# First two projection streams on x times the norm weight, with the token's factor applied when the sums are evacuated

## The reference, cut to what matters

```python
def rms_norm(x, g):
    xf = x.astype(jnp.float32)
    y = xf * lax.rsqrt(jnp.mean(xf * xf, axis=-1, keepdims=True) + EPS)
    return (y * g.astype(jnp.float32)).astype(x.dtype)
...
        h = rms_norm(x, norm_g[l])
        proj = h @ w_in[l]
        q, kv, g_logits, z_a, uv, z_b, merge_logits = jnp.split(proj, SPLIT_IDX, axis=-1)
```

## Time and profile before

| | |
|---|---|
| median of three runs | 2229.52 us |
| the profiled execution's own time | 2230.15 us |
| its span | 2228.4 us |
| TensorE busy | 2199.2 us (99%) |
| VectorE busy | 1545.2 us (69%) |
| ScalarE busy | 1080.6 us (48%) |
| GpSimd busy | 417.1 us (19%) |
| mean DMA rate | 173 GB/s |

### The profile page before, as it was taken

One profiled execution on the slowest core, in us unless ns is written; L12 is line 12 of the kernel. 1 busy time (PEld: TensorE's weight loads), 2 busy tenths in 40 slices (PEclk: granted clock), 3 DMA queues, 4 the chain that ended last, 5 costly groups with the idle time before them and its releaser, 6 DMA issues.

```text
span 2228.4 us, 42797 instructions
## 1 busy us (share of the span) xinstructions
PE 2199.2 (99%) x18366; PEld 2159.9 (97%) x18366; DVE 1545.2 (69%) x2588; ACT 1080.6 (48%) x1593; POOL 417.1 (19%) x331
## 2 busy tenths in 40 slices
PE   7999999999999999999999999999999999999998
PEld 7999999999999999999999999999999999999998
DVE  5555666664565567669999988899846447777564
ACT  4345555554544455344333666554545444444443
POOL 5110000000000000088878300570001011100000
PEclk9999999999999999999999999999999999999999
DMA  7766545656556665555555566566555555555652
GB/s 225 191 116 188 152 152 178 187 164 194 176 188 188 189 189 171 162 164 164 184 167 180 175 173 179 162 190 189 177 180 171 157 161 171 167 160 154 208 188 95
DMA packets 378791, 385.86 MB, mean 173 GB/s; under 512 B 14086, under 2 KB 371862, under 8 KB 378408
## 3 DMA queue, kind: packets, MB, share of 16 engines
q1 hardware_dynamic: 374394, 378.54, 55.8%
q0 software_dynamic: 2464, 3.21, 1.5%
q10 hardware_dynamic: 1744, 1.38, 0.2%
HBM read 380.72 MB, written 4.12 MB: 173 GB/s over the span
## 4 chain that ended last, share of the span: by engine, by line
PE 91%; DVE 4%; DMA 2%; ACT 1%; issue 1%; SPq 1%; POOL 0%; ACTq 0%; DVEq 0%
PE ps L461 28%; PE ps L471 28%; PE ps L466 28%; DMA raw<-in_w_in_dram 2%; DVE wlo L412 1%; PE ps L2611 1%; PE ps L2660 1%; ACT whi L405 1%; PE ps L2456 1%; PE ps L2640 0%; PE ps L2427 0%; PE ps L2439 0%; PE ps L2680 0%; DVE op_lo L547 0%; DVE arena L1963 0%
## 5 line engine op out<-in xcount | busy, mean ns | idle before, releaser
L405 ACT ACTIVATE whi<-raw 128x1024 fp32r<-128x1024 f32 (+1 forms) x688 | 723.7, 1057 | 878.4 <-PE ps L471 840.7
L412 DVE TENSOR_TENSOR wlo<-raw,whi 128x1024 fp32r<-128x1024 f32 x554 | 672.8, 1223 | 472.9 <-ACT whi L405 472.0
L461 PE MATMUL ps<-op_hi,whi 128*128 128x256 f32 (+1 forms) x5440 | 786.6, 287 | 5.0 <-DVE op_lo L1395 4.2
L466 PE MATMUL ps<-op_lo,whi 128*128 128x256 f32 (+1 forms) x5440 | 773.0, 284 | 1.1 <-DVE op_lo L1714 0.6
L471 PE MATMUL ps<-op_hi,wlo 128*128 128x256 f32 (+1 forms) x5440 | 771.8, 284 | 0.3 <-POOL wlo L412 0.3
L461 PEld LDWEIGHTS ps<-op_hi,whi 128*128 128x128 f32 x5440 | 705.9, 188 | 14.6 <-issue 6.6
L466 PEld LDWEIGHTS ps<-op_lo,whi 128*128 128x128 f32 x5440 | 706.8, 188 | 1.9 <-DVE op_lo L547 1.0
L471 PEld LDWEIGHTS ps<-op_hi,wlo 128*128 128x128 f32 x5440 | 706.3, 188 | 0.6 <-POOL wlo L412 0.5
L412 POOL TENSOR_TENSOR wlo<-raw,whi 128x1024 fp32r<-128x1024 f32 x134 | 332.4, 2491 | 1051.3 <-ACT whi L405 1050.9
L1847 DVE SCALAR_TENSOR_TENSOR ps<-arena,param_cols,ps 128x257 f32<-128x257 f32 (+6 forms) x448 | 183.3, 490 | 0.4
L1529 DVE SCALAR_TENSOR_TENSOR arena<-arena,nslopes,ps 128x128 f32<-128x128 f32 (+1 forms) x64 | 23.5, 410 | 48.2 <-PE ps L2427 46.4
(11 more groups left out here) (386 smaller groups left out, 1404.2 us busy)
## 6 DMA issues: line engine op xcount, KB each, us to landing
raw<-in_e_w_in_dram SPq DMA_DIRECT2D x96, 1024.0 KB, 5.4
raw<-in_w_in_dram SPq DMA_DIRECT2D x84, 1024.0 KB, 5.3
raw<-in_o_w_in_dram SPq DMA_DIRECT2D x64, 1024.0 KB, 5.8
raw<-in_e_w_out_dram SPq DMA_DIRECT2D x32, 1024.0 KB, 5.3
raw<-in_w_out_dram SPq DMA_DIRECT2D x16, 1024.0 KB, 5.3
raw<-in_w_ple_gate_dram SPq DMA_DIRECT2D x16, 1024.0 KB, 5.3
raw<-in_o_w_out_dram SPq DMA_DIRECT2D x16, 1024.0 KB, 5.3
arena<-cum_rows SPq DMA_DIRECT2D x16, 544.0 KB, 6.4
```

The lines of the kernel that those rows point to most:

```text
L405: nc.scalar.activation(half_view(whi[c % 2], c, n), half_view(raw[c % RING], c, n), ACT.Copy).then_inc(hi_ready, 1)
L412: own.tensor_tensor(half_view(wlo[c % 2], c, n), half_view(raw[c % RING], c, n), half_view(whi[c % 2], c, n).bitcast(F), ALU.subtract).the ...
L461: nc.tensor.matmul(o, hi8[c % 2][:, k, n * P:(n + 1) * P], MH[:, t, off:off + NT], start=(i % cpp == 0 and k == 0 and not (joint and n)), ...
L466: nc.tensor.matmul(o, hi8[c % 2][:, k, n * P:(n + 1) * P], ML[:, t, off:off + NT], start=False, stop=False, skip_group_check=joint)
```

## The change

The products of `kvc` and `qa` are no longer made with the normalized x but with x times the norm weight. For each of 16 tiles ScalarE takes the high part straight from the turned x in PSUM, scaled by the weight (`x_split_hi`), and VectorE the low part (`x_split_lo`). The token's factor is applied when the four pairs of sums are evacuated (`x_evac`), now on VectorE instead of ScalarE. The factor is made later, and its two products with ones stand between chunks 1 and 2. `h1` is still made for the streams from `qb` on, out of the residual into four new areas, and takes the place of the first operand behind chunks 6 and 7. The x parts come in another order (both halves of the tokens, then the next columns), the parameter loads move from behind chunk 1 to behind chunk 4, their turning from behind `kvc` to behind `qa`, and there is one fill product more. Four semaphores of GpSimd become one that counts.

```diff
-FILL = 4
+FILL = 5
...
+        X_BANK = (0, 4, 2, 6)
+        X_PARTS = [(tt, half) for half in range(2) for tt in range(2)]
...
             def load_params(i):
-                if i != 1:
+                if i != 0:
                     return
...
-            load_stream(sp_eng, "kvc", between=load_params)
-            for n in ("qa", "qb", "kvs"):
+            load_stream(sp_eng, "kvc")
+            load_stream(sp_eng, "qa", between=load_params)
+            for n in ("qb", "kvs"):
...
+            def x_split_hi(g_):
+                act.wait_ge(S("h1_psum"), g_ + 2)
+                for t in range(4 * g_, 4 * g_ + 4):
+                    nc.scalar.activation(MH[:, t, 0:S1], x_psum(g_)[:, t % 4, :], ACT.Copy, scale=GC[:, t:t + 1]).then_inc(S("xh_ready"), 1)
+
+            x_square(0)
+            x_square(1)
+            act.wait_ge(S("x_diag"), 1)
+            x_split_hi(0)
+            x_split_hi(1)
             split_hi(act, 0, 0)
+            x_split_hi(2)
+            split_hi(act, 0, 1)
+            x_split_hi(3)
+            split_hi(act, 1, 0)
+            split_hi(act, 1, 1)
+            x_square(2)
+            x_square(3)
+            act.wait_ge(S("factor_ms"), 2)
+            nc.scalar.activation(ms[:, 6:8], ms[:, 4:6], ACT.Sqrt).then_inc(S("factor_rt"), 2)
...
+            def h1_hi(g_):
                 act.wait_ge(src_ready, g_ + 1)
-                nc.scalar.activation(op(MH, S1)(g_), h1_psum(g_), ACT.Copy).then_inc(mh_ready, 1)
...
+                act.wait_ge(half_done, 2 * ST["qa"].end - 2 if g_ < 2 else 2 * ST["qa"].end)
+                nc.scalar.activation(op(MH, S1)(g_), H1[g_], ACT.Copy).then_inc(mh_ready, 1)
...
+            side("kvc")
+            side("qa", pre=h1_early)
+            h1_hi(2)
+            h1_hi(3)
+            act.wait_ge(acc_free, ST["qb"].p0)
...
+            x_split_lo(0)
+            raw_copy(0)
+            x_split_lo(1)
+            x_split_lo(2)
+            x_split_lo(3)
+            raw_copy(1)
+            raw_copy(2)
+            raw_copy(3)
...
+            def x_evac(base, scale):
+                def evac(j, par):
+                    V.scalar_tensor_tensor(out=qkvT[:, base + 2 * j:base + 2 * j + 2, :], in0=ps[:, pairof(par), 0:S1], scalar=scale,
+                                           in1=rstd[:, 0:S1].unsqueeze(1).to_broadcast([P, 2, S1]), op0=ALU.mult, op1=ALU.mult) \
+                        .then_inc(acc_free, 1)
+                return evac
+
+            def h1_first(i):
+                if i == 3:
+                    h1_scale(0)
+                    h1_scale(1)
+
+            def h1_rest(i):
+                if i < 2:
+                    h1_scale(2 + i)
+                if i == 3:
+                    h1_lo(0)
+                    h1_lo(1)
...
-            side("kvc", extra=raw_x)
-            side("qa", extra=key_blocks)
+            side("kvc", x_evac(8, 1.0), extra=h1_first)
+            side("qa", x_evac(0, HD ** -0.5), pre=h1_rest, extra=key_blocks)
+            h1_lo(2)
+            h1_lo(3)
...
+            def rstd_rows():
+                pe.wait_ge(S("x_diag"), 3)
+                pe.wait_ge(S("xT_copied"), 4)
+                for tt in range(2):
+                    mm = T.matmul(ps[:, 6, P * tt:P * tt + P], ones[:, :], DG[:, tt], start=True, stop=True)
+                mm.then_inc(S("h1_psum"), 1)
...
+            for c in range(ST["qa"].end):
+                for n in range(2):
+                    multiply_x(c, n)
+                if c == 1:
+                    rstd_rows()
+            raw_x(3)
+            stream_pe(pe, "qb", need="h1", hi=1)
             pe.wait_ge(S("pc_ready"), 4)
-            stream_pe(pe, "qb", hi=1)
             hidden(0)
```

More of the change, by code:

```diff
@@ L574, in _ @@
             nc.sync.dma_start(NGR[0:DT], A["norm_g"].rearrange("a (t n) -> (a t) n", t=DT)).then_inc(S("norm_g_landed"), 16)
[L575 to L576 removed]
+            for part, (tt, half) in enumerate(X_PARTS):
+                cols = slice(1024 * half, 1024 * half + 1024)
                 nc.sync.dma_start(xnat[:, tt, cols], A["x"][0, P * tt:P * tt + P, cols]).then_inc(S(f"x_landed_{part}"), 16)
             def load_params(i):
[L579 removed]
+                if i != 0:
                     return
@@ L1408, in _ @@
[L1408 to L1419, removed]
@@ L2315, in _ @@
+            for part, (tt, half) in enumerate(X_PARTS):
                 pe.wait_ge(S(f"x_landed_{part}"), 16)
[L2316 to L2323, removed]
+                if part == 2:
+                    pe.wait_ge(S("x_diag"), 1)
+                for t in range(8 * half, 8 if half == 0 else 12):
+                    mm = x_turn(t, tt)
+                    if tt == 1 and t % 4 == 3:
@@ L2324, in _ @@
                         mm.then_inc(S("h1_psum"), 1)
-            for tt in range(2):
-                pe.wait_ge(S("x_diag"), tt + 2)
-                T.matmul(ps[:, 7, S1 + P * tt:S1 + P * tt + P], ones[:, :], DG[:, tt], start=True, stop=True).then_inc(S("h1_psum"), 1)
-            pe.wait_ge(S("x_diag"), 4)
             for i in range(FILL):
                 T.matmul(ps[:, 7, S1:2 * S1], ident[:, :], xnat[:, 0, S1 * i:S1 * i + S1], start=True, stop=True)
-            for tt in range(2):
-                mm = x_turn(DT - 1, tt)
+            for t in range(12, DT):
+                for tt in range(2):
+                    mm = x_turn(t, tt)
@@ L2333, in _, with multiply_x, tile_wait @@
             mm.then_inc(S("h1_psum"), 1)
+            def rstd_rows():
+                pe.wait_ge(S("x_diag"), 3)
+                pe.wait_ge(S("xT_copied"), 4)
+                for tt in range(2):
+                    mm = T.matmul(ps[:, 6, P * tt:P * tt + P], ones[:, :], DG[:, tt], start=True, stop=True)
+                mm.then_inc(S("h1_psum"), 1)
+            def multiply_x(c, n):
+                p = c // 2
+                o = ps[:, 2 * (p % 2) + n, 0:S1]
+                if p >= 2 and c % 2 == 0 and n == 0:
+                    pe.wait_ge(acc_free, p - 1)
+                if c == 0 and n == 0:
+                    pe.wait_ge(S("xT_copied"), 1)
+                def tile_wait(sem, t):
+                    if c < 2 and n == 0:
+                        pe.wait_ge(S(sem), t + 1)
+                pe.wait_ge(hi_ready, 2 * c + n + 1)
+                for k in range(8):
+                    t = 8 * (c % 2) + k
+                    tile_wait("xh_ready", t)
+                    T.matmul(o, hi8[c % 2][:, k, n * P:(n + 1) * P], MH[:, t, 0:S1], start=(c % 2 == 0 and k == 0), stop=False)
+                for k in range(8):
+                    t = 8 * (c % 2) + k
+                    tile_wait("xl_ready", t)
+                    T.matmul(o, hi8[c % 2][:, k, n * P:(n + 1) * P], ML[:, t, 0:S1], start=False, stop=False)
+                lo_wait(pe, c, n)
+                for k in range(8):
+                    mm = T.matmul(o, lo8[c % 2][:, k, n * P:(n + 1) * P], MH[:, 8 * (c % 2) + k, 0:S1], start=False,
+                                  stop=(c % 2 == 1 and k == 7))
+                mm.then_inc(half_done, 1)
```

112 lines of the change are left out of this document (51 added, 61 removed).

## The result

| | before | after |
|---|---|---|
| median | 2229.81 us (6 runs) | 2236.52 us (6 runs) |
| ratio, 95% interval | | 1.0031, 1.002 to 1.0041 |
| profiled execution, its span | 2230.15, 2228.4 us | 2237.06, 2235.3 us |
| small products behind chunk 8 start | 75.89 us | 84.56 us |

The change made the kernel 6.7 us **slower**. I had forecast 2228.5, in a range that ended at 2233.5. The last row of the table is the mark by which all kernels here are compared: the 32 small products, which stand behind chunk 8 in each kernel. TensorE's place in the program is 8.7 us later there, and 6.9 us later at the end of the span; so nearly all of it comes about in the first 85 us.

A forecast was written before the change was run, and what follows sets the result against it. TensorE was taken as busy throughout, leaving only the start, bound by chunk 2's late transfer, to gain from. 8.9 - 6.6 - 1.3 = 1.0 us faster than 2230.15, median 0.6 below that: 2228.5, range 2223.2 to 2233.5.

The forecast's parts named there:

- Gross gain 8.9: At the head, the shorter path to the first operand starts chunk 2 at 26.2 instead of 35.1, 8.9 us earlier.
- rival 3: Head not shortened: first tiles or diagonals 5 us late, gross gain 4, same time; chance 0.03.
- VectorE's chain: VectorE's in-order work from chunk 5's landing to the h1 low parts chunk 8 needs: 26.0 us, delaying TensorE 6.6.
- The floor of 2.6: Before chunk 8, VectorE's work after chunk 6 takes 9.7 against TensorE's 7.1, so 2.6 us are lost for certain.
- If chunk 6 lands with its end, at 52, its high half is ready at 53.1: Chunk 6 meeting GpSimd's earlier loads: VectorE, there at 51.2, would lose 1.9 us; chunk 8 as much again.
- I take 1.3 of 0 to 3.8: Loss assumed for GpSimd's earlier loads meeting chunks 6 to 8: 1.3 us, bounds 0 to 3.8.
- a full queue: Reason given for SyncE's 13.47 us issue of chunk 3 in the kernel before.
- Chunk 5: Behind the 13 parameter loads: 24.8 for chunk 4 plus 17.6 makes 42.4, taken as 42.1; at most 0.1 us lost there.
- SyncE's long issue: Sign that the forecast is right: SyncE's issue of some 13 us would now stand at chunk 6.
- Rival 2: Waits at chunks 6 and 8 cost two clock drops of about 3.4 us each: 5.8 slower, 2234.9; chance 0.10.
- Rival 1: Parameters no obstacle, chunk 5 lands before 38.1: only the floor's 2.6 us lost, 6.3 faster, 2223.2; chance 0.19.
- My premise that chunk 2 sets the end before: In the kernel before, chunk 2 effectively starts at 35.1 and TensorE never waits after 36.99, so that moves the end.

The follow-up runs named there:

- e8: The changed kernel with the 31-row load cut into 16 and 15, the key blocks one chunk earlier and x in its old order: 2220.4 us, ratio 0.996.
- e7: The changed kernel with the 13 parameter loads back behind chunk 1, uncut: 2235.18 us, ratio 1.0025 to the kernel before.
- e1: The changed kernel with the 31-row parameter load cut into loads of 16 and 15 rows: 2224.83 us, ratio 0.9984 to the kernel before.
- e2: The changed kernel with GpSimd's compression loads held back until chunk 6 has landed, 31 rows uncut: 2229.46 us, ratio 1.0001 to the kernel before.
- e4: The changed kernel with 5 fill products ahead of chunk 5 and 15 ahead of chunk 6: 2236.91 us, ratio 1.0034 to the kernel before.
- e9: The changed kernel with only VectorE's eight key block operations moved one chunk earlier, 31 rows uncut: 2235.3 us, ratio 1.0024 to the kernel before.
- e6: The kernel of e1 with VectorE's eight key block operations moved one chunk earlier in its order: 2222.19 us, ratio 0.9964 to the kernel before.
- e5: The kernel before, without the change, with the 31-row load cut into 16 and 15: 2228.86 us, ratio 0.9997.
- e3: The kernel of e1 with GpSimd's loads also set to wait for chunk 6, which held nothing back: 2224.86 us, ratio 0.9978 to the kernel before.

## Why the prediction was wrong

**The head was right.** Gross gain 8.9 by my sum, 8.2 measured; first product 14.53 for 13.9, chunk 2 at 26.94 for 26.2. The difference is x: its first part landed at 6.11, 0.7 later than before, because the change also loads it in another order (e8, with the old order: 5.54). I had counted the tiles from before's start. The clock was full from the first product, as expected, so rival 3 was out.

**VectorE's chain and the floor were right.** From ScalarE's start on chunk 6 at 59.77, my terms give 1.1 for the high half and 26.0 - 9.1 = 16.9 for the rest: 77.8, and the fifth product of chunk 8 started at 77.76. The floor of 2.6 was 2.7 in e7.

**The step that failed** is "If chunk 6 lands with its end, at 52, its high half is ready at 53.1", and with it "I take 1.3 of 0 to 3.8". Chunk 6 landed at 59.8, nearly 8 us beyond the upper end. With 59.8 in my own sum, chunk 8's fifth product comes at 77.8 rather than 61.5 when unhindered, 16.3 late; 8.9 - 16.3 is 7.4 slower, 2236.9 against 2236.52 measured. I had bounded the collision by the mean rate of a stretch of before (50 to 62, share 1.26 for 187 GB/s). That was the wrong figure: chunk 8, which was issued at 46.10 and met GpSimd's loads there, needed 15.9 us to land at 62.03. With 3.0 us each for chunks 7 and 8 it would have been there by 52.1, an estimate; it came 9.9 us later, and in e1 10.8 later, reckoned in the same way. That GpSimd's loads are what held it up there is argued, since no run takes them away from chunk 8; for chunk 6 e2 shows it. In the changed kernel it is chunk 6 that had not landed when they began (at 38.20; I had said 36), since chunk 5 ahead of it was held up behind the 31 rows: chunk 6 went from 46.8 (e2) to 59.8, and TensorE was due at it at 54.0. The other 2 to 3 us of the 13.0 stay open, and so does the way in which the transfers meet. The 13.47 us for which SyncE was busy with one issue, which I put down to a full queue, moved along as well, to 14.44; before and e7 (14.08) have it with the 31 rows in front, e2 has no issue above 5.56, and what holds the issue no run shows.

**Chunk 5** landed at 45.66, not 42.1. e2 shows 43.82 without GpSimd's loads: 1.7 us of the error are there without them, since 17.6 was carried over from a start with other starting conditions. How much of the rest is the same collision can't be told, as the same loads gave 44.42 in e4 and 48.29 in e9. SyncE's long issue came at chunk 8 (14.44), not at chunk 6.

**Rival 2** named nearly the right time, 2234.9 (its 5.8 slower make 2235.3 by my own sum), for a wrong reason, so that is luck. Three drops of the clock came, of 1.4 to 1.6 us each rather than 3.4 (the table above), but e4 took two of them away and won nothing. Its condition, "chunk 6 landing after about 50", was met, and the price lay in the wait itself. **Rival 1** needed the 31 rows out of the way: e1, where only the floor and the slow sets behind it are lost, gave 2224.8 for its 2223.2, and e6, with the key blocks also moved, 2222.2. My premise that chunk 2 sets the end before held only in part: freeing it moved the mark by 1.0 us and the time by nothing that can be told (e5).

## What to carry to other kernels

When a change moves a load that runs on one DMA engine, ask which transfers will now still be in flight when the next group of loads begins, from every engine that issues them, and price the meeting by how long a single chunk took from issue to landing in such a stretch, not by the mean rate; better, cut the load so that it spreads, and only then judge the move. When a transfer is late for an engine that works in order, the next operand behind it follows at a fixed distance; compute that distance first, since fills, clock and moved operations inside it changed little here. An edit that is worth next to nothing alone (the cut, before) can decide what another one is worth.

## What was not expected of the hardware

- GpSimd's loads move little, but a chunk that is in flight beside them lands late: 16.8 us behind its issue in e1 and 15.9 in the kernel before, where the median is 5.3, and chunk 6 of the changed kernel 13.0 us later than in e2. How the transfers meet inside the DMA engines no run here shows.
- The wait before chunk 8 was 1.98 + 0.33 in e7 and 1.89 + 0.34 in e3, yet the next set took 0.95 in e7 (granted clock 1.00 from 76 to 78) and 1.71 in e3 (0.50 from 66 to 68), whose row in TensorE's timeline is

```profile
65.85 1.91 PE L470 MATMUL ps<-op_lo,whi 128*128 128x256 f32 x8
```

  Why a pause of the same length costs the clock in one kernel and not in the other stays open.
